# Routing of head 0 indexed alone, eleven early u tiles, heads 1 to 3 indexed together

## What is computed

```python
q  = (xt @ w_q).reshape(n_tok, 8, 2, 128)                # 256 tokens, 8 heads, 2 halves
sc = einsum("thcd,hckd->thck", q, sub_keys)              # 128 keys for each half
top_s, top_i = top_k(sc, 16)
cand_s = top_s[:, :, 0, :, None] + top_s[:, :, 1, None, :]
cand_e = top_i[:, :, 0, :, None] * 128 + top_i[:, :, 1, None, :]
best_s, best_j = top_k(cand_s, 16); experts = take_along_axis(cand_e, best_j)
gates = softmax(best_s)
h    = einsum("thkd,td->thk", u_tab[experts], x)         # 128 rows of u for each token
coef = gates * gelu(h)
out  = einsum("thk,thkd->td", coef, v_tab[experts])
```

## Time and profile before

| | us |
|---|---|
| median of 3 runs | 3293.93 (3290.31 to 3294.55) |
| the profiled execution | 3297.1 |
| its span in the trace | 3295.4 |
| TensorE busy | 2879.7 (87%) |
| VectorE busy | 2466.0 (75%) |
| GpSimd busy | 1557.6 (47%) |
| ScalarE busy | 825.6 (25%) |
| DMA | 1108.20 MB, mean 336 GB/s |

### The profile page before, as it was taken

One profiled execution on the slowest core, in us unless ns is written; L12 is line 12 of the kernel. 1 busy time (PEld: TensorE's weight loads), 2 busy tenths in 40 slices (PEclk: granted clock), 3 DMA queues, 4 the chain that ended last, 5 costly groups with the idle time before them and its releaser, 6 DMA issues.

```text
span 3295.4 us, 44606 instructions
## 1 busy us (share of the span) xinstructions
PE 2879.7 (87%) x15107; PEld 2210.8 (67%) x15107; DVE 2466.0 (75%) x3641; ACT 825.6 (25%) x1274; POOL 1557.6 (47%) x1313
## 2 busy tenths in 40 slices
PE   9999987667777899999899999977768777999998
PEld 8887887666777644444697977966667776444443
DVE  6996698999999766666533555898899988766666
ACT  1014432113433500000233534422224335200000
POOL 0000567767677644444200002777676777544443
PEclk9999998888988999999999999988789889999999
DMA  8434499999999899999765334799999999999998
GB/s 259 153 128 153 150 362 422 421 421 412 419 417 421 309 410 406 409 409 402 267 211 179 129 138 156 258 409 421 422 422 416 416 419 353 376 410 405 409 407 344
DMA packets 293996, 1108.20 MB, mean 336 GB/s; under 512 B 22068, under 2 KB 120948, under 8 KB 220788
## 3 DMA queue, kind: packets, MB, share of 16 engines
q0 software_dynamic: 147456, 805.37, 60.3%
q1 hardware_dynamic: 146420, 301.26, 25.3%
HBM read 1104.45 MB, written 2.10 MB: 336 GB/s over the span
## 4 chain that ended last, share of the span: by engine, by line
DMA 39%; PE 27%; DVE 15%; issue 9%; POOL 7%; ACT 2%; SPq 0%; POOLq 0%; DVEq 0%; ACTq 0%
DMA ring<-in_peer_u,index_now 17%; DMA work<-in_peer_v,index_add 13%; PE ps L865 6%; DMA more_add<-in_peer_v,index_add 6%; PE ps L762 5%; DVE ring L1870 5%; POOL ring L604 5%; PE ps L805 5%; DVE ps L1942 3%; PE ps L816 2%; DMA work<-in_peer_v,index_v 2%; PE ps L944 1%; PE ps L1048 1%; DMA ring<-in_peer_w_q 1%; PE ps L1026 1%
## 5 line engine op out<-in xcount | busy, mean ns | idle before, releaser
L604 POOL DMA_INDIRECT ring<-in_peer_u,index_now x480 | 793.0, 1652 | 343.9 <-issue 137.9
L1870 DVE SCALAR_TENSOR_TENSOR ring<-ring,x_tok 128x2048 f32<-128x2048 f32 x372 | 843.4, 2289 | 102.8 <-DMA ring<-in_peer_u,index_now 101.5
L1101 PE MATMUL ps<-all_v,mix 128*128 128x512 f32 x1984 | 851.8, 592 | 0.0
L1101 PEld LDWEIGHTS ps<-all_v,mix 128*128 128x128 f32 x1984 | 377.0, 190 | 474.5 <-issue 474.5
L1054 PE MATMUL ps<-x_dot,work 128*128 128x128 f32 x3968 | 524.9, 296 | 113.3 <-DVE ps L1877 73.1
L1942 DVE SCALAR_TENSOR_TENSOR ps<-work,coef,ps 128x1024 f32<-128x1024 f32 x326 | 419.0, 1288 | 244.9 <-DMA work<-in_peer_v,index_add 202.6
L1054 PEld LDWEIGHTS ps<-x_dot,work 128*128 128x128 f32 x3968 | 502.4, 209 | 142.9 <-ACT work L1404 72.2
L588 POOL TENSOR_TENSOR w_lo<-ring,w_hi 128x512 fp32r<-128x512 f32 x104 | 134.0, 1324 | 829.2 <-ACT w_hi L1234 804.9
L1404 ACT ACTIVATE work<-ps 128x1024 f32<-128x1024 f32 x248 | 243.6, 1022 | 611.2 <-PE ps L1048 610.7
L1632 DVE TENSOR_TENSOR w_lo<-ring,w_hi 128x2048 fp32r<-128x2048 f32 x85 | 194.8, 2292 | 246.9 <-ACT w_hi L1234 246.8
L714 POOL DMA_INDIRECT work<-in_peer_v,index_add x256 | 242.0, 945 | 268.2 <-DVE ps L1942 220.5
(11 more groups left out here) (234 smaller groups left out, 3811.9 us busy)
## 6 DMA issues: line engine op xcount, KB each, us to landing
all_v<-in_peer_v SPq DMA_DIRECT2D x248, 512.0 KB, 6.8
ring<-in_peer_w_q SPq DMA_DIRECT2D x16, 2048.0 KB, 9.4
ring<-in_attn_w_kv SPq DMA_DIRECT2D x16, 2048.0 KB, 8.7
ring<-in_conv_w_in SPq DMA_DIRECT2D x14, 2048.0 KB, 9.0
ring<-in_conv_w_out SPq DMA_DIRECT2D x8, 2048.0 KB, 7.4
ring<-in_attn_w_q SPq DMA_DIRECT2D x8, 2048.0 KB, 8.2
ring<-in_attn_w_o SPq DMA_DIRECT2D x8, 2048.0 KB, 7.3
ring<-in_peer_u,index_now POOLq DMA_INDIRECT x480, 13.7
```

The source lines that it names most:

```text
L604: pool.indirect_dma_start(tile, None, u_tab, bass.IndirectOffsetOnAxis(ap=index_now[:, half, s:s + 1], axis=0)).then_inc(landed_in, 16)
L1101: mm = pe.matmul(ps[:, dense_bank(tb, q), :], mix[tb][:, row, :], tile[:, q * 512 - HALF:(q + 1) * 512 - HALF], start=False, stop=True, sk ...
L1870: dve.scalar_tensor_tensor(out=tile, in0=tile, scalar=1.0, in1=x_tok[:, tb, :], op0=ALU.mult, op1=ALU.mult, accum_out=coef[:, tb, slot]).t ...
```

## The change

The index is made for head 0 alone first, then for heads 1 to 3 together (before: heads 0 and 1, then 2 and 3). Eleven tiles go through the four rooms (before: eight); the three new ones are slots 1, 2, 3 of group 1, which the ring then leaves out. GpSimd splits halves 0 to 5 and 7 first and VectorE takes half 6. The gathers stand at other places between GpSimd's halves, the early dots at other places between VectorE's. ScalarE copies x to PSUM one half later. GpSimd waits for the index of heads 1 to 3 before groups 2 and 3. The diff, without the parts that only carry slot numbers and semaphore counts along:

```diff
-EARLY = 8
+EARLY = 11
+EARLY_PLACES = (1, 2, 3)
...
         def early_landed(layer, e):
-            return (layer * (EARLY // ROOMS) + e // ROOMS + 1) * 16
+            uses = -(-(EARLY - e % ROOMS) // ROOMS)
+            return (layer * uses + e // ROOMS + 1) * 16
+        def early_slot(e):
+            return e if e < U_RING else U_RING + EARLY_PLACES[e - U_RING]
...  # GpSimd
                 def gather_first(first, last):
                     for s in range(first, last):
-                        gather_row(u_tile(s), U_RING + s, u_row[s])
+                        if s not in EARLY_PLACES:
+                            gather_row(u_tile(s), U_RING + s, u_row[s])
...
-                for u in range(8):
+                for u in range(6):
                     split_half(U_WQ[layer] + u)
                 pool.wait_ge(route[layer], part_done(0, 0))
-                gather_early(0, 3)
+                gather_early(0, ROOMS)
+                next_half(7)
+                gather_early(ROOMS, ROOMS + 1)
                 next_half(9)
-                gather_early(3, 5)
+                gather_early(ROOMS + 1, ROOMS + 3)
                 next_half(11)
-                gather_early(5, 7)
+                gather_early(ROOMS + 3, ROOMS + 5)
                 next_half(13)
-                gather_early(7, EARLY)
+                gather_early(ROOMS + 5, EARLY)
...
                 gather_first(4, U_RING)
+                pool.wait_ge(route[layer], part_done(0, 1))
                 for group in (2, 3):
                     gather_group(0, group, group % 2)
...  # ScalarE
                     if m == 1:
                         take_keys()
+                    if m == 2:
                         act.wait_ge(sk_taken, 4 * (layer + 1))
                         act.activation(ps[:, Q:2 * Q, :]..., x_tok[:, 0, :], ACT.Copy)
...  # VectorE
                     for s in range(first, last):
-                        if s not in TURNED:
+                        if s in EARLY_PLACES:
+                            dve.sem_inc(u_used, 1)
+                        elif s not in TURNED:
                             dot(0, u_tile(s), ...)
...
-                for h in range(2):
-                    route_keys(layer, 0, h, h + 1)
-                    route_pairs(layer, 0, h, h + 1)
-                part_numbers(layer, 0, 0, 2)
+                route_keys(layer, 0, 0, 1)
+                route_pairs(layer, 0, 0, 1)
+                part_numbers(layer, 0, 0, 1)
                 for c in range(2):
-                    part_key(layer, 0, 0, 2, c)
-                part_index(layer, 0, 0, 2)
+                    part_key(layer, 0, 0, 1, c)
+                part_index(layer, 0, 0, 1)
+                route_keys(layer, 0, 1, 2)
+                next_half(6)
+                route_pairs(layer, 0, 1, 2)
+                early_dots(0, 3)
                 next_half(8)
-                route_keys(layer, 1, 0, 2)
-                early_dots(0, 2)
+                early_dots(3, 6)
+                route_keys(layer, 0, 2, 4)
                 next_half(10)
-                route_keys(layer, 0, 2, 4)
-                early_dots(2, 3)
+                early_dots(6, 8)
                 route_pairs(layer, 0, 2, 4)
+                early_dots(8, 9)
                 next_half(12)
-                early_dots(3, 5)
+                early_dots(9, EARLY)
                 route_keys(layer, 0, 4, 6)
                 next_half(14)
-                early_dots(5, 7)
+                part_numbers(layer, 0, 1, 4)
+                for c in range(2):
+                    part_key(layer, 0, 1, 4, c)
+                part_index(layer, 0, 1, 4)
                 route_pairs(layer, 0, 4, 6)
-                early_dots(7, EARLY)
-                part_numbers(layer, 0, 2, 4)
-                for c in range(2):
-                    part_key(layer, 0, 2, 4, c)
-                part_index(layer, 0, 2, 4)
+                route_keys(layer, 1, 0, 2)
                 first_dots(0, U_RING // 2)
```

More of the change, by code:

```diff
@@ L47 @@
 LN_HEAD = 9
-ROUTING = (("keys", 0, 0, 1), ("pairs", 0, 0, 1), ("keys", 0, 1, 2), ("pairs", 0, 1, 2), ("part", 0, 0, 2),
-           ("keys", 1, 0, 2), ("keys", 0, 2, 4), ("pairs", 0, 2, 4), ("keys", 0, 4, 6), ("pairs", 0, 4, 6), ("part", 0, 2, 4),
+ROUTING = (("keys", 0, 0, 1), ("pairs", 0, 0, 1), ("part", 0, 0, 1), ("keys", 0, 1, 2), ("pairs", 0, 1, 2),
+           ("keys", 0, 2, 4), ("pairs", 0, 2, 4), ("keys", 0, 4, 6), ("part", 0, 1, 4), ("pairs", 0, 4, 6), ("keys", 1, 0, 2),
            ("keys", 0, 6, 8), ("pairs", 0, 6, 8), ("logits", 0, 0, 8), ("part", 0, 4, 8), ("gate", 0, 0, 8),
@@ L116, in build @@
     PANELS = 8
-    assert TB == 2 and KC == 16 and Q == 4 and NKEY == P and DQ == P and HC == KC and EARLY == U_RING
+    assert TB == 2 and KC == 16 and Q == 4 and NKEY == P and DQ == P and HC == KC and EARLY == U_RING + len(EARLY_PLACES)
     P_OUT, P_WQ = 2 * PANELS, [3 * PANELS, 8 * PANELS]
@@ L371, in ring_group, with row_at @@
             return layer * RING_GROUPS + tb * GROUPS - 1
-        def row_at(layer, tb):
-            return (ring_group(layer, tb) + 1) * 16
+        def row_at(layer, tb, s):
+            skipped = layer + 1 if s in EARLY_PLACES else 0
+            return (ring_group(layer, tb) + 1 - skipped) * 16
         def turned_banks(h):
@@ L638, in gather_early @@
                             pool.wait_ge(early_used, layer * EARLY + e - ROOMS + 1)
-                        gather_row(early_tile(e), e, early_row[e % ROOMS])
+                        gather_row(early_tile(e), early_slot(e), early_row[e % ROOMS])
                 def gather_first(first, last):
                     for s in range(first, last):
-                        gather_row(u_tile(s), U_RING + s, u_row[s])
+                        if s not in EARLY_PLACES:
+                            gather_row(u_tile(s), U_RING + s, u_row[s])
                 def next_half(u):
@@ L667, in _ @@
                 gather_first(4, U_RING)
+                pool.wait_ge(route[layer], part_done(0, 1))
                 for group in (2, 3):
                     gather_group(0, group, group % 2)
-                for tb, first, group, pairs in ((0, 2, 4, 2), (0, 4, 8, 4), (1, 0, 0, 4), (1, 4, 8, 4)):
+                for tb, first, group, pairs in ((0, 1, 4, 2), (0, 4, 8, 4), (1, 0, 0, 4), (1, 4, 8, 4)):
                     pool.wait_ge(route[layer], part_done(tb, first))
@@ L1042, in turned_dots @@
                         n = ring_group(layer, tb) * NT + e
-                        pe.wait_ge(u_row[s], i * 16 + row_at(layer, tb))
+                        pe.wait_ge(u_row[s], i * 16 + row_at(layer, tb, s))
                         for h in range(2):
@@ L1887, in early_dots @@
                         dve.scalar_tensor_tensor(out=tile, in0=tile, scalar=1.0, in1=early_x(e),
-                                                 op0=ALU.mult, op1=ALU.mult, accum_out=coef[:, 0, e:e + 1]).then_inc(early_used, 1)
+                                                 op0=ALU.mult, op1=ALU.mult, accum_out=coef[:, 0, early_slot(e):early_slot(e) + 1]).then_inc(early_used, 1)
                 def dots(tb, first, last):
@@ L1898, in dots @@
                             else:
-                                dot(tb, u_tile(s), u_row[s], i * 16 + row_at(layer, tb), bass.ds(i * U_RING + s, 1))
+                                dot(tb, u_tile(s), u_row[s], i * 16 + row_at(layer, tb, s), bass.ds(i * U_RING + s, 1))
                 def half_group(tb, group, half):
@@ L1910, in half_group @@
                             slot = group * U_RING + s
-                            dot(tb, u_tile(s), u_row[s], group * 16 + row_at(layer, tb), slice(slot, slot + 1))
+                            dot(tb, u_tile(s), u_row[s], group * 16 + row_at(layer, tb, s), slice(slot, slot + 1))
                 def last_dot(tb, e):
@@ L1921, in first_dots @@
                     for s in range(first, last):
-                        if s not in TURNED:
-                            dot(0, u_tile(s), u_row[s], 16 + row_at(layer, 0), slice(U_RING + s, U_RING + s + 1))
+                        if s in EARLY_PLACES:
+                            dve.sem_inc(u_used, 1)
+                        elif s not in TURNED:
+                            dot(0, u_tile(s), u_row[s], 16 + row_at(layer, 0, s), slice(U_RING + s, U_RING + s + 1))
                 def opening_dots():
@@ L1930, in opening_dots @@
                         else:
-                            dot(1, u_tile(s), u_row[s], row_at(layer, 1), slice(s, s + 1))
+                            dot(1, u_tile(s), u_row[s], row_at(layer, 1, s), slice(s, s + 1))
                 def weights(tb):
```

## The result

The changed kernel takes 3366.14 us, median of 4 runs (3361.97 to 3374.74), beside 3293.01 for the kernel before (4 runs, 3290.31 to 3294.55). The ratio is 1.0229, with a 95% interval of 1.0217 to 1.0242: 73 us slower, where 61 were forecast (3355, range 3330 to 3372). The profiled execution took 3364.93 us, its span is 3363.2.

A forecast was written before the change was run, and what follows sets the result against it. DMA bytes were taken to bound the u stage, TensorE the projection before it. Per layer 29.0 + 2.7 - 1 = 30.7, in all 61.4 on 3297.1 gives 3358.5, for the median 3355 us; range 3330 to 3372.

The forecast's parts named there:

- three turns of waits: Projection: VectorE's halves 10, 12, 14 wait for tiles gathered behind GpSimd's halves 9, 11, 13; half 14 29.0 us late.
- the stage behind them: Stage of u tiles after the projection: time is DMA bytes, 244 tiles x 1.049 MB / 0.42 = 609 us.
- the signs given for the profile: Expected between 420 and 490 us: VectorE waits of 5 to 9 us, TensorE idle stretches of about 7, 10 and 11.
- the lower bound: Projection with every landing at 5.5 us and start at 411.0: half 10 at 431.3, half 14 at 475.7, 22.4 us late.
- The tile count: Tiles asked for ahead of the projection's end: 12 before and after; a better filled stage start wins 1 us a layer.
- The slow clock: TensorE at half clock after the third stall: 2.7 us a layer on the path, between 0 and 5.
- the start: Ahead of the first turn: third tile lands about 407, dot 2 ends 409.3, half 8 ends 411.5, as before.
- the stage pays half of it back: Rival: VectorE, not DMA, paces the stage behind the projection; some +16 us a layer, 3326; chance 0.08 including shorter turns.
- The much slower rival of 40 us a layer: GpSimd's halves stretch beside VectorE's index work, landings take 11 us, slow clock paid in full; 3374 and over; chance 0.07.
- three tiles leave the saturated stage: Faster rival, first 80 us after the projection: 6.6 or 7.5 us a layer won, 13 to 15 in all, 3280; chance 0.04.
- The new wait for the index of heads 1 to 3: GpSimd after the projection's end: index ready at 495, GpSimd there about 498; costs nothing, 0 to 3 us.
- VectorE isn't the limit of the stage as a whole: Stage behind the projection: VectorE 19.4 to 19.7 us busy of 20 at first, 91 of 100 later at the same DMA rate.

The follow-up runs named there:

- the kernel before with half 14 late: The kernel before, with eight unused sums over x (some 2.2 us each) on VectorE ahead of half 14: 3325.1 us, ratio 1.011.
- the run with fifteen tiles: The kernel with both edits, plus head 1's own index and three group 2 tiles asked for before the projection ends: 3306.2 us.
- the last two runs: On the kernel with both edits: all early dots from PSUM, VectorE's dots of places 5 to 7 right after the index; fifteen tiles 3313.4 us, twelve 3312.3.
- the kernel with both edits: The changed kernel with dots gathered behind odd halves moved behind the next even half, and gathers 2 and 3 behind half 7: 3309.2 us.

## Why the prediction was right, and where it was off

**The mechanism** was as forecast: three turns of waits, the stage behind them unchanged. Both ends of it were moved by experiments, and either took the turns away. In the changed kernel they took, from the end of one of VectorE's halves to the end of the next, 23.9, 23.9 and 23.7 us (413.6, 437.5, 461.4, 485.1); the working had 23.4, 23.6 and 23.85. Landings beside a panel were 8.8 and 8.6 us (8.4 taken), without one 5.5 and then 7.3 (5.5 and 7.6 taken). Two of the signs given for the profile were off although the turns were right: VectorE's three waits were 9.7, 11.6 and 10.7 us and not 5 to 9 (the terms of the sum themselves leave 9.2, 11.4 and 10.7), and TensorE's idle stretches were 7.1, 8.9 and 8.7 us and not 7, 10 and 11, since the passes at the low clock fill part of the later two. In the lower bound the terms add up to 431.5 for half 10 and not 431.3, which changes nothing.

**The tile count** held: 12 tiles ahead of the end in both, and the u stage 619.1 before, 618.0 after in layer 0, where 1 us was taken as won. In layer 1 no gain shows (617.8 and 618.0).

**The slow clock** after the third stall: from the w_lo pass of half 14 to the first gather 11.2 us instead of 8.1, so 3.1 where 2.7 was taken.

**The term that was mis-sized is the start.** The prediction let half 8 end at 411.5 and said that dot 2 sets it. It worked out that four gathers and one panel, 6.3 MB, take 15 us on the DMA engines, and used that for the third tile only; the panel is in the same 6.3 MB, it came last, and ScalarE can't round halves 8 and 9 without it. The 15 us were short too: the next panel (401.3) and gather 4 (402.0) went out before this panel had landed, and from 390.0 to 409.2 the DMA engines moved 7.5 MB. The panel landed 20.5 us after its issue, 9.4 before. Dot 2 had started at 405.2 and was done at 407.5, so it wasn't what set half 8. Half 8 ended at 413.6, which is 47.1 us after the w_lo pass of half 1 and not 41.8 as taken: 5.3 us a layer. With 0.7 from the turns and 0.4 from the clock that is the difference between the 31.7 forecast and the 38.0 measured. The run with gathers 2 and 3 behind half 7 shows why it can't be won back alone: dot 2 then sets VectorE's half 8 to the same place, 47.4 us.

**The sum.** 38.0 in layer 0 and 38.7 in layer 1 (from its half 3 on) make 76.7; 73 were measured between the medians and 67.8 between the two profiled spans. The spans differ by some 3 us each in two stretches whose code the change doesn't touch, ahead of layer 0's projection and ahead of layer 1's. The first of them, up to the w_lo pass of half 1, ends between 366.2 and 369.9 us in the twelve profiled executions, so 3 us is what it varies by; no run shows why. So it is no merit of the working that the measured difference lies 12 us over the forecast's 61 and not 15.

**The rivals.** That the stage pays half of it back fell with its 619.1 and 618.0 us, and the kernel before with half 14 late put a price on it: nothing is absorbed. The much slower rival of 40 us a layer was nearer than its chance of 0.07 says, since 38.0 and 38.7 were measured. Its reasons weren't there: no half of GpSimd was stretched in the changed kernel's three turns (5.0 us each), and the landings in them that VectorE waited for took 5.5 to 8.8 us. The late start brought the time so close. That three tiles leave the saturated stage fell by the count in the changed kernel. Where three more truly were early, in the run with fifteen tiles, the stage was no shorter either, and GpSimd waited for the ring's places. The new wait for the index of heads 1 to 3 cost nothing, as said: the index was ready at 497.0, GpSimd got there at 501.

**What I called right without testing it** is that VectorE isn't the limit of the stage as a whole. Later in the stage it is 91 us busy of 100 at the same DMA rate, but in its first 60 to 80 us it is as full as the DMA engines are, and in the last two runs another order of its work there made the stage 5.9 us longer.

## What to carry to other kernels

When two engines hand work to each other in written-out orders, put both lists side by side and follow each item from its request to its use: a transfer asked for behind the partner's step k and awaited ahead of one's own step k + 1 puts its whole landing time into every turn, and moving either end by one step takes it out (here 25 to 28 us of a layer's 38). Count how many tiles have been asked for when the late stage begins before counting a prefetch as won, and count the places that the next ones need. A burst of gathers also delays what the other queue has under way, so look for who waits for that transfer, not only for the gathers.

## What the runs showed of the hardware

GpSimd's subtraction of 128x2048 fp32 took 9.1 us instead of 5.05 beside VectorE dots with both operands in SBUF, and 5.05 beside the same dots with x in PSUM; VectorE's dots, 2.3 us otherwise, took up to 3.4 there. Either engine can be the one that pays: with fifteen tiles GpSimd's half 15 in layer 0 took its usual 5.03 us, and the dot beside it 7.64.

```profile
454.59 7.64 DVE L1904 SCALAR_TENSOR_TENSOR ln_rows<-ln_rows,x_tok 128x2048 f32<-128x2048 f32 x1 [0.38 <-DMA ln_rows<-in_peer_u,index]
...
455.04 5.03 POOL L595 TENSOR_TENSOR w_lo<-ring,w_hi 128x512 fp32r<-128x512 f32 x4
```

A 2 MB panel load issued 0.6 us ahead of the first of four 1 MB gathers landed last of the five, 20.5 us after its issue, where it took 9.4 with nothing beside it. With only two gathers right behind it, in the kernel with both edits, it took 14.6. I had expected it to keep its place.
